# GpSimd takes 384 of 1024 columns of the modulation's sums during the first mixer

## The chip, the core and the metric

The kernel runs on one core of a Trainium2 chip. The metric is the device time of one execution in microseconds, as the median of several runs.

## The reference

The program is a chain of three transformer blocks on a sequence of 256 positions and 1024 channels, all in float32. The first block is conditioned on a vector c by a modulation of six rows:

```
c_act = silu(c)
mod = einsum('bd,de->be', c_act, w_ada) + b_ada          # w_ada: 1024 x 6144
shift_m, scale_m, gate_m, shift_f, scale_f, gate_f = split(mod, 6)
h = rms(x) * (1 + scale_m) + shift_m
proj = h @ w_in                                          # q, k, v, gates of two mixers
fox = forgetting attention, 8 heads of 64;  ret = retention, 4 heads of 128
x = x + gate_m * (concat(fox, ret) @ w_out)
h = rms(x) * (1 + scale_f) + shift_f
x = x + gate_f * (square(relu(h @ w_mlp_in)) @ w_mlp_out)
```

Two further blocks follow (sparse attention with pooling, and gated linear attention), each with its own MLP. The change touches only the product of c_act with w_ada.

## The kernel before

The weights stream from memory in tiles of 128 partitions by 1024 columns (512 KB) through the tensor raw, which has six slots (RAW = 6). The list RAW_SEQ, made by raw_plan, sets the one order in which all tiles pass: ("w", s) is tile s of a weight matrix, ("ada", n) is row block n of w_ada. For a weight tile ScalarE copies raw to whi (hi_to, L581), VectorE writes the rest to wlo (L1107), and TensorE multiplies with both (L1766 to L1768). SyncE (SP) issues the transfers in the order of the list; slot_wait lets tile r go only when raw_done says that tile r - 6 has been used. ScalarE and VectorE work three tiles ahead of TensorE (LEAD = 3).

The modulation is not a TensorE product. For each row block n of w_ada VectorE does one scalar_tensor_tensor (L1130): sums = raw * c_act[block] + sums, where sums is one of six 1024-column pieces of acc. Blocks 0 to 15 (the first two rows of the modulation, in halves, L1117 to L1126) come before the first projections. Blocks 16 to 39 follow one at a time, one behind each weight tile from tile 12 to tile 35; that is the stretch of the first mixer. Blocks 40 to 47 come in the first MLP. When a modulation row's eight blocks are in, mod_bcast on TensorE adds up the partitions (L1854) and ScalarE writes the row back (L609).

Each engine runs its own program in order and waits on semaphores. Between the tiles of w_in the engines do the steps of the mixer, at places fixed by tables (`tiles(T_IN, T_OUT, {...})` on ScalarE and VectorE, `between` on TensorE). On the path of the prediction are: heads_out on ScalarE (L785, the turned and scaled heads; two stand right behind the copy of tile 16), fox_scores on TensorE (L1992, which for the first group waits for four of them), rotate on VectorE (L1390 to L1395) and turn on TensorE (L2110), and quarters of the normalised mixer output (L1757).

GpSimd has little to do. It clears acc, kT and qT, issues a number of transfers (sel, const_c, the gains, decay_c, bands_c, layer norm rows), and computes inverse roots as powers of -1/2 (rsqrt, L467) of up to eight columns, which VectorE asks for (var_ready) and waits for (rstd_ready).

Of the kernel before, what the change touches and what calls it, by code (L numbers as in the profile page):

```python
# [9 lines left out]
ALU = mybir.AluOpType  # L10
AX = mybir.AxisListType.X

P = 128
D = 1024
S = 256
NT = S // P
KC = D // P
# [8 lines left out]
RAW = 6  # L26
# [32 lines left out]

ADA_ORDER = [1, 0, 2, 4, 3, 5]  # L60
ADA_FIRST = 2 * KC


ADA_AFTER = list(range(12, 36))
# [21 lines left out]
ADA_AT = [r for r, (kind, n) in enumerate(RAW_SEQ) if kind == "ada"]  # L86


def raw_full_at(r):

    return 16 * sum(2 if RAW_SEQ[a][0] == "ada" and RAW_SEQ[a][1] < ADA_FIRST else 1 for a in range(r % RAW, r + 1, RAW))


def raw_of(s):
# [4 lines left out]
def units(n):  # L99

    return 4 * (n - 1) - (4 if n > 4 else 0)
# [67 lines left out]
def block_program(nc, dram, out):  # L169
    with ExitStack() as ctx:  # L170
        def sb(name, shape, dt=F32):
            return ctx.enter_context(nc.sbuf_tensor(name, shape, dt))

        def sem(name):
            return ctx.enter_context(nc.semaphore(name))
# [8 lines left out]
        acc = sb("acc", [P, 6 * D])  # L184
# [16 lines left out]
        cvec = sb("cvec", [P, 4, KC])  # L201
# [17 lines left out]
        cred = sb("cred", [P, 4, 16])  # L219
        aT = sc[0:32, 1, 0:S]  # L220
        dec = sb("dec", [P, 4, 4])

        PJ = ctx.enter_context(nc.psum_tensor("PJ", [P, 4, 512], F32))
        AT = ctx.enter_context(nc.psum_tensor("AT", [P, 4, 512], F32))
# [14 lines left out]
        acc_zero, ld_bada, ld_bada2 = sem("acc_zero"), sem("ld_bada"), sem("ld_bada2")  # L239
        xn_done, xt_tr, xt_done, modc_done = sem("xn_done"), sem("xt_tr"), sem("xt_done"), sem("modc_done")  # L240
        h0_hi, h0_32, h0_lo = sem("h0_hi"), sem("h0_32"), sem("h0_lo")
        ada_even = sem("ada_even")
        exp_c = sem("exp_c")
        cast_done = sem("cast_done")
        mod_mm, mod_row = sem("mod_mm"), sem("mod_row")
# [105 lines left out]
        def _(sp):  # L351
            def slot_wait(r):

                if r >= RAW:
                    sp.wait_ge(raw_done, r - RAW + 1)

            def fetch(r, src, view=None):

# [102 lines left out]
        def _(pool):  # L461
            asked = [0]

            def rsqrt(col, n):
                asked[0] += 1
                pool.wait_ge(var_ready, asked[0])
                nc.gpsimd.tensor_tensor(rstd[:, col:col + n], stat[:, col:col + n], nhalf[:, 0:n],  # L467
                                        ALU.pow).then_inc(rstd_ready, 1)
# [25 lines left out]
            bcast(fgain, dram["fox_out_gain"].rearrange("a h d -> (a h d)")).then_inc(ld_mix, 16)  # L494
            bcast(rgain, dram["ret_out_gain"].rearrange("a h d -> (a h d)")).then_inc(ld_mix, 16)
            pool.dma_start(tab[:, 0:1024], dram["decay_c"]).then_inc(ld_mix, 16)
            for t in range(NT):
                rsqrt(S_FO + 8 * t, 8)
            for t in range(NT):
                rsqrt(S_RO + 4 * t, 4)  # L500
            pool.wait_ge(src_ready, units(2))
            pool.dma_start(tab[:, :], dram["bands_c"]).then_inc(ld_tab, 16)

# [576 lines left out]
        def _(dve):  # L1080
# [19 lines left out]
            def raw_to(end):  # L1100

                while nxt[0] < end:
                    r = nxt[0]
                    kind, n = RAW_SEQ[r]
                    if kind == "w":
                        dve.wait_ge(hi_done, n + 1)
                        tt(wlo[:, n % SPL, :], raw_slot(r), whi[:, n % SPL, :].bitcast(F32),  # L1107
                           ALU.subtract).then_inc(raw_done, 1)
                    else:
                        dve.wait_ge(raw_full[r % RAW], raw_full_at(r))  # L1110
                        before, last_ada[0] = last_ada[0], r
                        if n < ADA_FIRST:
                            g, q = divmod(n, 4)
                            even, odd = acc[:, 512 * g:512 * (g + 1)], prT[:, g % 2, :]
                            if q:
                                dve.wait_ge(ada_even, n)
                            stt(even, raw_slot(r)[:, 0:512], cvec[:, 3, 2 * q:2 * q + 1], even, ALU.mult, ALU.add)\  # L1117
                                .then_inc(ada_even, 1)
                            c = cvec[:, 3, 2 * q + 1:2 * q + 2]
                            if q == 0:  # L1120
                                if g >= 2:
                                    dve.wait_ge(mod_mm, g - 1)
                                ts(odd, raw_slot(r)[:, 512:], c, None, ALU.mult).then_inc(raw_done, 1)
                            else:
                                dve.wait_ge(raw_done, before + 1)
                                stt(odd, raw_slot(r)[:, 512:], c, odd, ALU.mult, ALU.add).then_inc(raw_done, 1)  # L1126
                        else:
                            dve.wait_ge(raw_done, before + 1)
                            sums = acc[:, ADA_ORDER[n // KC] * D:(ADA_ORDER[n // KC] + 1) * D]
                            stt(sums, raw_slot(r), cvec[:, 3, n % KC:n % KC + 1], sums, ALU.mult, ALU.add)\  # L1130
                                .then_inc(raw_done, 1)
                    nxt[0] += 1

# [613 lines left out]
        def _(pe):  # L1747
# [101 lines left out]
            def mod_bcast(n, bank0):  # L1849

                pe.wait_ge(raw_done, ADA_AT[KC * n + KC - 1] + 1)
                i = ADA_ORDER[n]
                for j in range(2):
                    ins = mm(AT[:, bank0 + j, :], cst[:, C_TRI + P:C_TRI + 2 * P],  # L1854
                             acc[:, i * D + 512 * j:i * D + 512 * (j + 1)], start=True, stop=True)
                    ins.then_inc(mod_mm, 1)
# [645 lines left out]
```

## Time and profile before

| | |
|---|---|
| median of 3 runs | 1022.15 us |
| the runs | 1015.5, 1022.15, 1022.82 us |
| profiled execution | 1015.01 us, span 1013.2 us |
| TensorE busy | 951.8 us (94%) |
| VectorE busy | 656.6 us (65%) |
| ScalarE busy | 485.2 us (48%) |
| GpSimd busy | 53.9 us (5%) |

The span is what the profiler saw from the first to the last instruction; the execution's own time has 1.8 us around it. Busy shares are means over stages with different limits, so they name no bottleneck by themselves. TensorE's matmuls overlap, and their ends are modelled. "Idle before" is the time an engine stood still ahead of an instruction, with the one that released it.

### The profile page before, as it was taken

The page shows a single profiled execution, that of the slowest core. Times are in us where ns is not written, and L with a number is a line of the kernel's source. Part 1 is how long each engine was busy: PE and PEld are TensorE (multiplying, and loading weights), DVE is VectorE, ACT ScalarE, POOL GpSimd, SP SyncE. Part 2 cuts the span into 40 slices and gives each one's busy share as a digit, 9 for nine tenths or more (in the row PEclk, how much of TensorE's full clock was granted, in tenths as well). Part 3 has the DMA queues.
Part 4 walks back from the last instruction along what each step waited for, and adds up shares of the span by engine and source line. Part 5 has one row for each costly group of instructions (what it writes and reads, how often), then busy time and mean ns, then how long its engine had stood idle before and what let it go on. Part 6 is the DMA issues. An engine that isn't in the chain of part 4 may idle for free.

```text
span 1013.2 us, 14870 instructions
## 1 busy us (share of the span) xinstructions
PE 951.8 (94%) x5572; PEld 816.1 (81%) x5572; DVE 656.6 (65%) x828; ACT 485.2 (48%) x734; POOL 53.9 (5%) x59
## 2 busy tenths in 40 slices
PE   3889979799999999999899999998999989999996
PEld 3767867599999987977689999996776879999995
DVE  5778897886545575666884555558544876554555
ACT  5456646455444444444354544443653735444540
POOL 3030101100000001000020000001000010000000
PEclk9999989999999999999999999999999999999998
DMA  9998776776665576411476556544442447566531
GB/s 285 300 244 287 206 205 231 254 239 220 198 198 185 167 268 153 134 67 59 125 214 230 167 186 201 193 167 147 144 149 100 125 167 249 171 198 206 172 125 42
DMA packets 109991, 186.94 MB, mean 184 GB/s; under 512 B 8696, under 2 KB 67088, under 8 KB 109920
## 3 DMA queue, kind: packets, MB, share of 16 engines
q1 hardware_dynamic: 104800, 177.33, 54.2%
q0 software_dynamic: 2592, 8.53, 3.0%
q8 instruction: 34, 0.56, 0.2%
q10 hardware_dynamic: 2544, 0.35, 0.2%
q14 instruction: 21, 0.17, 0.0%
HBM read 185.13 MB, written 1.05 MB: 184 GB/s over the span
## 4 chain that ended last, share of the span: by engine, by line
PE 78%; DVE 9%; ACT 4%; issue 3%; DMA 2%; POOL 2%; SPq 0%; POOLq 0%; ACTq 0%; DVEq 0%
PE PJ L1766 14%; PE PJ L1767 13%; PE PJ L1768 13%; PE AT L1908 9%; PE AT L1907 9%; PE AT L1906 9%; DVE wlo L1107 2%; POOL rstd L467 2%; PE AT L1992 1%; DMA raw<-in_w_out_dram 1%; PE AT L2035 1%; PE AT L1757 1%; DMA raw<-in_w_in_dram 1%; DVE bn L1192 1%; DVE acc L1130 1%
## 5 line engine op out<-in xcount | busy, mean ns | idle before, releaser
L1107 DVE TENSOR_TENSOR wlo<-raw,whi 128x1024 fp32r<-128x1024 f32 x144 | 172.7, 1220 | 53.4 <-ACT whi L581 52.9
L1906 PE MATMUL AT<-hT_hi,whi 128*128 128x256 f32 x720 | 203.8, 283 | 0.0
L1908 PE MATMUL AT<-hT_hi,wlo 128*128 128x256 f32 x720 | 203.8, 283 | 0.0
L1907 PE MATMUL AT<-hT_lo,whi 128*128 128x256 f32 x720 | 203.7, 283 | 0.0
L1235 DVE TENSOR_TENSOR wlo<-raw,whi 128x1024 fp32r<-128x1024 f32 x144 | 169.8, 1221 | 33.1 <-ACT whi L639 32.6
L1766 PE MATMUL PJ<-whi,uhi 128*128 128x512 f32 x432 | 170.3, 394 | 1.7 <-DVE wlo L1107 0.9
L581 ACT ACTIVATE whi<-raw 128x1024 fp32r<-128x1024 f32 x144 | 146.7, 1054 | 49.4 <-DMA raw<-in_w_in_dram 29.3
L1767 PE MATMUL PJ<-wlo,uhi 128*128 128x512 f32 x432 | 168.7, 390 | 0.0
L1768 PE MATMUL PJ<-whi,ulo 128*128 128x512 f32 x432 | 168.2, 389 | 0.0
L639 ACT ACTIVATE whi<-raw 128x1024 fp32r<-128x1024 f32 x144 | 144.4, 1049 | 48.2 <-PE PJ L1768 44.3
L1766 PE MATMUL PJ<-whi,hT_hi 128*128 128x512 f32 (+1 forms) x320 | 132.3, 413 | 11.4 <-DVE hT_lo L1283 7.3
L1906 PEld LDWEIGHTS AT<-hT_hi,whi 128*128 128x128 f32 x720 | 138.1, 192 | 1.6
L1907 PEld LDWEIGHTS AT<-hT_lo,whi 128*128 128x128 f32 x720 | 138.1, 192 | 1.6
L1908 PEld LDWEIGHTS AT<-hT_hi,wlo 128*128 128x128 f32 x720 | 138.0, 192 | 0.0
L1244 DVE TENSOR_TENSOR pr<-pr 128x512 f32<-128x512 f32 x45 | 31.1, 691 | 161.0 <-ACT pr L649 161.0
L1767 PE MATMUL PJ<-wlo,hT_hi 128*128 128x512 f32 (+1 forms) x320 | 125.2, 391 | 0.0
L1768 PE MATMUL PJ<-whi,hT_lo 128*128 128x512 f32 (+1 forms) x320 | 125.0, 391 | 0.0
L649 ACT ACTIVATE pr<-AT 128x512 f32<-128x512 f32 x45 | 26.8, 597 | 190.0 <-PE AT L1908 190.0
L1766 PEld LDWEIGHTS PJ<-whi,uhi 128*128 128x128 f32 x432 | 81.3, 188 | 20.1 <-issue 2.8
L1768 PEld LDWEIGHTS PJ<-whi,ulo 128*128 128x128 f32 x432 | 81.1, 188 | 17.3
L1767 PEld LDWEIGHTS PJ<-wlo,uhi 128*128 128x128 f32 x432 | 81.3, 188 | 15.2 <-issue 0.2
L1766 PEld LDWEIGHTS PJ<-whi,hT_hi 128*128 128x128 f32 x320 | 61.5, 192 | 30.1 <-DVE hT_lo L1283 8.7
(310 smaller groups left out, 1054.8 us busy)
## 6 DMA issues: line engine op xcount, KB each, us to landing
raw<-in_mlp_w_dram SPq DMA_DIRECT2D x128, 512.0 KB, 4.9
raw<-in_w_in_dram SPq DMA_DIRECT2D x32, 512.0 KB, 6.0
raw<-in_w_ada_dram SPq DMA_DIRECT2D x32, 512.0 KB, 5.0
raw<-in_w_mlp_in_dram SPq DMA_DIRECT2D x32, 512.0 KB, 5.0
raw<-in_w_mlp_out_dram SPq DMA_DIRECT2D x32, 512.0 KB, 5.4
raw<-in_c_w_in_dram SPq DMA_DIRECT2D x24, 512.0 KB, 4.3
raw<-in_w_ada_dram SPq DMA_DIRECT2D x32, 256.0 KB, 6.0
raw<-in_a_w_in_dram SPq DMA_DIRECT2D x12, 512.0 KB, 5.0
```

The lines of the kernel that those rows point to most:

```text
L581: nc.scalar.activation(whi[:, s % SPL, :], raw_slot(r), ACT.Copy).then_inc(hi_done, 1)
L639: nc.scalar.activation(whi[:, s % SPL, :], raw_slot(r), ACT.Copy).then_inc(hi_done, 1)
L649: nc.scalar.activation(pr[:, 0, :], AT[:, j % 2, :], ACT.Relu).then_inc(relu_done, 1)
L1107: tt(wlo[:, n % SPL, :], raw_slot(r), whi[:, n % SPL, :].bitcast(F32), ALU.subtract).then_inc(raw_done, 1)
L1235: tt(wlo[:, s % SPL, :], raw_slot(r), whi[:, s % SPL, :].bitcast(F32), ALU.subtract)\
L1244: tt(pr[:, 1, :], pr[:, 0, :], pr[:, 0, :], ALU.mult).then_inc(usq, 1)
L1766: mm(o, a, hi, start=start, stop=False)
L1767: mm(o, a, lo, start=False, stop=False)
L1768: return mm(o, b, hi, start=False, stop=stop)
L1906: mm(o, whi[:, s % SPL, c], hT_hi[:, k, :], start=first, stop=False, skip_group_check=True)
L1907: mm(o, whi[:, s % SPL, c], hT_lo[:, k, :], start=False, stop=False, skip_group_check=True)
L1908: ins = mm(o, wlo[:, s % SPL, c], hT_hi[:, k, :], start=False, stop=last, skip_group_check=True)
```

## The change

For blocks 16 to 39 VectorE now sums only columns 0 to 639. GpSimd does columns 640 to 1023 with two instructions, since it has no single one for both: share = raw * c_act[block], then sums = sums + share. A new tensor share of 128 x 512 is allocated. A new semaphore ada_pool counts finished shares, ada_prod the products. SP fetches into a slot that held such a block only when both engines are done with it, and TensorE waits for both before it adds up a row. The inverse roots that GpSimd does in this stretch are placed between the shares.

```diff
+ADA_CUT = 640
+ADA_SHARED = range(2 * KC, 5 * KC)
...
+def shared_to(r):
+
+    return sum(1 for n in ADA_SHARED if ADA_AT[n] <= r)
...
                 if r >= RAW:
                     sp.wait_ge(raw_done, r - RAW + 1)
+                    if shared_to(r - RAW) > shared_to(r - RAW - 1):
+                        sp.wait_ge(ada_pool, shared_to(r - RAW))
...
-            for t in range(NT):
-                rsqrt(S_FO + 8 * t, 8)
+            pool.wait_ge(ld_bada2, 16)
+
+            def ada_share(n0, n1):
+
+                for n in range(n0, n1):
+                    r, k = ADA_AT[n], n - ADA_SHARED[0]
+                    pool.wait_ge(raw_full[r % RAW], raw_full_at(r))
+                    if k:
+                        pool.wait_ge(ada_pool, k)
+                    col = ADA_ORDER[n // KC] * D
+                    sums = acc[:, col + ADA_CUT:col + D]
+                    nc.gpsimd.tensor_scalar(share[:, 0:D - ADA_CUT], raw_slot(r)[:, ADA_CUT:],
+                                            cvec[:, 3, n % KC:n % KC + 1], None, ALU.mult).then_inc(ada_prod, 1)
+                    pool.wait_ge(ada_prod, k + 1)
+                    nc.gpsimd.tensor_tensor(sums, sums, share[:, 0:D - ADA_CUT], ALU.add).then_inc(ada_pool, 1)
+
+            ada_share(16, 26)
+            rsqrt(S_FO, 8)
+            ada_share(26, 30)
+            rsqrt(S_FO + 8, 8)
+            ada_share(30, 37)
             for t in range(NT):
                 rsqrt(S_RO + 4 * t, 4)
+            ada_share(37, 40)
...
-                            sums = acc[:, ADA_ORDER[n // KC] * D:(ADA_ORDER[n // KC] + 1) * D]
-                            stt(sums, raw_slot(r), cvec[:, 3, n % KC:n % KC + 1], sums, ALU.mult, ALU.add)\
+                            cut = ADA_CUT if n in ADA_SHARED else D
+                            sums = acc[:, ADA_ORDER[n // KC] * D:ADA_ORDER[n // KC] * D + cut]
+                            stt(sums, raw_slot(r)[:, 0:cut], cvec[:, 3, n % KC:n % KC + 1], sums, ALU.mult, ALU.add)\
...
+                if KC * n in ADA_SHARED:
+                    pe.wait_ge(ada_pool, KC * (n - 1))
```

On GpSimd, from the powers of the q and k heads to the next block's tables, the program before reads as follows (L467 are the powers, L471 broadcasts of a gain row):

```order
L467 TENSOR_TENSOR rstd<-stat,nhalf 128x8 [waits var_ready] x4
L493 DMA cst<-in_const_c_dram 128x512 [waits mod_mm]
L471 DMA acc<-in_fox_out_gain_dram 128x512
L471 DMA tab<-in_ret_out_gain_dram 128x512
L496 DMA tab<-in_decay_c_dram 128x1024
L467 TENSOR_TENSOR rstd<-stat,nhalf 128x8 [waits var_ready] x2
L467 TENSOR_TENSOR rstd<-stat,nhalf 128x4 [waits var_ready] x2
L502 DMA tab<-in_bands_c_dram 128x1536 [waits src_ready]
```

and in the changed program, up to its second share:

```order
L477 TENSOR_TENSOR rstd<-stat,nhalf 128x8 [waits var_ready] x4
L503 DMA cst<-in_const_c_dram 128x512 [waits mod_mm]
L481 DMA acc<-in_fox_out_gain_dram 128x512
L481 DMA tab<-in_ret_out_gain_dram 128x512
L506 DMA tab<-in_decay_c_dram 128x1024
L518 TENSOR_SCALAR share<-raw,cvec 128x384 [waits raw_full5,ld_bada2]
L521 TENSOR_TENSOR acc<-acc,share 128x384 [waits ada_prod]
L518 TENSOR_SCALAR share<-raw,cvec 128x384 [waits ada_pool,raw_full1]
L521 TENSOR_TENSOR acc<-acc,share 128x384 [waits ada_prod]
```

The first share stands behind the four powers and the four transfers; ten shares then run ahead of the next power.

On SP, the transfers from the tile of sum 16 on in the changed program (L371 is the fetch, L361 before; before, all of these wait for raw_done alone):

```order
L371 DMA raw<-in_w_ada_dram 128x1024 [waits raw_done]
L371 DMA raw<-in_w_in_dram 128x2x512 [waits raw_done]
L371 DMA raw<-in_w_ada_dram 128x1024 [waits ada_pool,raw_done]
L371 DMA raw<-in_w_in_dram 128x2x512 [waits raw_done]
L371 DMA raw<-in_w_ada_dram 128x1024 [waits ada_pool,raw_done]
L371 DMA raw<-in_w_in_dram 128x2x512 [waits raw_done]
```

From the tile of sum 19 on, each w_ada tile waits for GpSimd too, and the weight tile behind it stands in the same queue.

## Rows read from the trace of the kernel before

**Rows 1.** The page, part 1: busy us, share of span, instructions

```profile
PE 951.8 (94%) x5572; PEld 816.1 (81%) x5572; DVE 656.6 (65%) x828; ACT 485.2 (48%) x734; POOL 53.9 (5%) x59
```

**Rows 2.** Table of stretches: length, then each engine's busy us, clock, DMA share

```profile
95.00:115.00 20.00, 20.00 (x119) 17.59 (x118) 13.54 (x16) 13.38 (x36) 0.00 (x0) 1.00 0.90 232
115.00:143.00 28.00, 22.76 (x111) 17.82 (x110) 26.85 (x41) 17.50 (x25) 4.64 (x2) 0.95 0.65 199
...
205.00:400.00 195.00, 193.87 (x1211) 174.79 (x1209) 120.89 (x122) 90.57 (x111) 4.12 (x3) 1.00 0.63 203
```

**Rows 3.** Tile raw, 60 to 205 us: duration ns min/median/max, first and last start

```profile
L1130 DVE SCALAR_TENSOR_TENSOR acc<-raw,cvec,acc x24: 1273/1276/1285, 69.2 to 177.6; 128x1024 f32<-128x1024 f32 x24
...
DMA to landing us min/median/max: 3.2/5.4/10.2
```

**Rows 4.** Tile acc, 0 to 420 us, the same columns

```profile
L1117 DVE SCALAR_TENSOR_TENSOR acc<-raw,cvec,acc x16: 733/742/750, 9.1 to 53.6; 128x512 f32<-128x512 f32 x16
```

**Rows 5.** GpSimd's instructions in time: start us, us, engine, line, operation

```profile
0.78 1.80 POOL L474 MEMSET acc<- 128x2048 f32 x1
7.38 0.55 POOL L467 TENSOR_TENSOR rstd<-stat,nhalf 128x1 f32<-128x1 f32 x1 [4.80 <-DVE stat L1161]
...
8.84 3.51 POOL L477 MEMSET acc<- 128x4096 f32 x1
...
77.45 0.54 POOL L496 DMA_DIRECT2D tab<-in_decay_c_dram  x1
115.45 2.63 POOL L467 TENSOR_TENSOR rstd<-stat,nhalf 128x8 f32<-128x8 f32 x1 [37.45 <-DVE stat L1161]
...
193.42 1.48 POOL L467 TENSOR_TENSOR rstd<-stat,nhalf 128x1 f32<-128x1 f32 x1 [16.14 <-DVE stat L1161]
```

**Rows 6.** VectorE's instructions in time

```profile
116.47 1.23 DVE L1107 TENSOR_TENSOR wlo<-raw,whi 128x1024 fp32r<-128x1024 f32 x1
117.62 0.68 DVE L1390 TENSOR_TENSOR sc<-PJ,cst 128x512 f32<-128x512 f32 x1
...
171.50 0.69 DVE L1226 SCALAR_TENSOR_TENSOR proj<-PJ,proj 128x512 f32<-128x512 f32 x1 [0.51 <-ACT proj L624]
...
193.25 1.22 DVE L1107 TENSOR_TENSOR wlo<-raw,whi 128x1024 fp32r<-128x1024 f32 x1
```

**Rows 7.** SP's issues in time

```profile
70.56 0.34 SPq L361 DMA_DIRECT2D raw<-in_w_ada_dram  x1
71.69 0.37 SPq L361 DMA_DIRECT2D raw<-in_w_in_dram  x1
```

**Rows 8.** ScalarE's instructions in time

```profile
80.53 1.06 ACT L581 ACTIVATE whi<-raw 128x1024 fp32r<-128x1024 f32 x1
81.61 1.26 ACT L785 ACTIVATE kT<-AT,qkgain 64x512 f32<-64x512 f32 x2
```

**Rows 9.** TensorE's instructions in time

```profile
84.20 1.05 PE L1992 MATMUL AT<-kT,qT 104*128 104x128 f32 x8
...
94.55 0.63 PE L2004 MATMUL AT<-cst,pr 128*128 128x128 f32 x4 [0.95 <-ACT kT L785]
...
140.70 1.08 PE L2110 MATMUL AT<-cst,proj 128*128 128x128 f32 x4 [4.03 <-DVEq L1396]
```

**Rows 10.** Table of stretches, two microseconds behind that idle time

```profile
142.00:144.00 2.00, 1.06 (x5) 1.10 (x6) 1.74 (x3) 0.42 (x1) 0.00 (x0) 0.50 0.03 8
```

**Rows 11.** The chain that ended last, 55 to 210 us: start us, us, what

```profile
176.56 8.72 DMA raw<-in_w_out_dram
```

**Rows 12.** Groups of VectorE's instructions, 115 to 143 us: busy us, mean ns, idle before

```profile
L1130 DVE SCALAR_TENSOR_TENSOR acc<-raw,cvec,acc 128x1024 f32<-128x1024 f32 x6 | 7.7, 1281 | 0.5 <-DVE proj L1395 0.5
L1107 DVE TENSOR_TENSOR wlo<-raw,whi 128x1024 fp32r<-128x1024 f32 x5 | 6.1, 1219 | 0.0
L1395 DVE TENSOR_TENSOR proj<-sc 128x512 f32<-128x512 f32 x4 | 2.8, 693 | 0.1
...
L1371 DVE TENSOR_TENSOR proj<-proj,acc 128x512 f32<-128x512 f32 x2 | 1.4, 692 | 0.1
```

More of the change, by code:

```diff
@@ L221, in block_program @@
         dec = sb("dec", [P, 4, 4])
+        share = sb("share", [P, 512])
         PJ = ctx.enter_context(nc.psum_tensor("PJ", [P, 4, 512], F32))
@@ L241, in block_program @@
         h0_hi, h0_32, h0_lo = sem("h0_hi"), sem("h0_32"), sem("h0_lo")
-        ada_even = sem("ada_even")
+        ada_even, ada_prod, ada_pool = sem("ada_even"), sem("ada_prod"), sem("ada_pool")
         exp_c = sem("exp_c")
```

## The prediction, made before the changed kernel ran

> **What bounds the kernel now.** The stage table of the page comes first: over the whole span VectorE is busy 65%, so its work as such buys nothing [rows 1]. The table of stretches says where it does: from 205 us on TensorE is busy 193.87 of 195.00 us, and from 95 to 115 us all of the time; only from 115 to 143 us does it stand at 22.76 of 28.00 while VectorE is at 26.85 [rows 2]. That is the first mixer. What is gained or lost there is passed on whole, because nothing behind 205 us has room to take it up or to give it back.
>
> Who waits there? TensorE has its one long idle time before 140.70 us, 4.03 us, and what ends it is VectorE (the rotated queries of retention) [rows 9]. The view of instructions in time shows VectorE working without a gap up to that point. So the modulation's sums (L1130) that it does on the way count in full in this stretch, and nearly nowhere else.
>
> **The change, part by part.**
>
> *VectorE's shorter instruction.* All 24 sums that start between 69.2 and 177.6 us shrink from 1024 to 640 columns. One takes 1276 ns at 1024 columns [rows 3], the 512-column form 742 ns [rows 4]. The slope is 534 / 512 = 1.04 ns a column, so 384 columns are 0.40 us; for 24 that is 9.6 us, the most that the change could ever bring, 0.9% of the span. Between 95 and 115 us TensorE hides it: cover, no gain. In 115 to 143 us six sums start, the last at the very end, and five lie ahead of the step TensorE waits for [rows 12]: **-2.0 us**. In the tail, the chain passes through the transfer of a w_out tile, which is issued at 176.56 us, when a sum frees its slot, and lands 8.72 us later [rows 11]: one sum, -0.4 us.
>
> *GpSimd's two instructions, 24 times.* The trace shows no large GpSimd arithmetic. Its nearest rows are the two memsets: 1.80 us for 2048 columns, 3.51 for 4096, or 0.835 ns a column written [rows 5]. 384 columns are 0.32 us for the product (one input). The sum has two inputs; if it reads them one after the other, 0.64 us (below: 0.32, if both come at once; above: twice that, 1.28). What stands around it: a power of one column takes 0.55 us with VectorE quiet [rows 5], of which I take 0.43 as fixed, since with VectorE in the way it ends 0.43 after the obstacle (next part). A share is thus 0.75 + 1.07 = 1.8 us, at a supply of one tile per 4 to 5 us. GpSimd keeps up, once it has started. The Trainium skill (GPSIMD Engine Reference, Performance versus the Vector engine) gives 4497 ns for an add of 2048 columns; scaled to 384 an estimate from it is 0.84 us, in place of my 0.64 and 0.43. No row here shows such an add.
>
> *The port.* The power of one column at 193.42 us took 1.48 us, not 0.55. VectorE ran a 1.22 us subtraction with both inputs in SBUF from 193.25 to 194.47; GpSimd ended 0.43 later [rows 5, 6]. So GpSimd does wait for such an instruction to end. The other direction is not so clear. At 115.45 an 8-column power waited in the same way and ran on to 118.08, while VectorE's next subtraction ran from 116.47 in its usual time (1.23 us) and its successor began 1.15 later, as always [rows 5, 6]. VectorE was not held while GpSimd computed; it can have been held for 8 reads at most, too little to see. With 384 columns the reads last as long as the instruction streams. I take it that GpSimd, once waiting, gets in between two VectorE instructions (as at 116.5) and holds the next two-input one while it reads: 0.32 + 0.64 = 0.96 us a share. How much of VectorE's time is exposed: L1130 5 x 1.28, L1107 6.1, L1395 2.8, and three groups of 1.4 us like L1371 have both inputs in SBUF [rows 12], together 19.5 of 28 us, 0.70. The eight shares 26 to 33 fall here: 8 x 0.70 x 0.96 = **+5.4 us** (bounds: 0, if both engines read side by side; 8 x 0.70 x 1.82 = +10.2, if the whole instruction holds the port).
> By the Trainium skill (SBUF — State Buffer, Who interferes with whom) whichever instruction starts first has the pair for the whole instruction. The row of GpSimd waiting agrees; the 8-column row, where VectorE ran beside it, does not. By that rule the term would be the +10.2 of the bound.
>
> *The late start.* This is the wait that the change adds on the queue of transfers. A slot is refilled only when GpSimd is through with it too. When VectorE has done sum 16, SP issues the tile of sum 19 into its slot, at 70.56 us, and tile 16 of w_in next, at 71.69 [rows 7]. But GpSimd's program reaches its first share only after two powers and four DMA issues, at 77.45 + 0.54 = 78.0 us [rows 5], some 0.4 earlier with the shorter sum ahead of the powers. With 1.8 us for the share and about 0.5 us before each of its halves for a VectorE instruction to end, SP gets on at 80.4, and tile 16, queued behind, is issued at 80.8: 9.1 us late. Landing takes 5.4 us in the median, 3.2 at least [rows 3]: 86.2. ScalarE's copy of that tile stands at 80.53 us [rows 8], and behind it on ScalarE stand the turned heads (81.61), without which TensorE's first attention scores at 84.20 can't start [rows 9]. From copy to heads done it is 2.34 us: scores at 88.5, 4.3 late. Of it the 0.95 us that TensorE later waits anyway (94.55) is taken back [rows 9]: **+3.4 us**. Below: with no port waits and a 3.2 us landing +0.3. The slack behind it does not swallow the rest, since 95 to 115 us is TensorE at its limit and VectorE's gapless stretch begins from what TensorE and ScalarE hand it. Above: after the idle 4.03 us the granted clock is 0.50 from 142 to 144 us, the 1.2 GHz level [rows 10]; a new idle time of that length could be followed by the same, and at half speed for 4 to 5 us cost some 2 us more.
>
> *The other moved steps.* The four inverse roots stand between shares now. The first is asked at 115.45 us [rows 5], and VectorE uses its result four tiles later in its program: hidden. Share 26 stands behind it and ends about 3 us after VectorE's own part, but the tile fetched into its slot is used six places later in the sequence: hidden too, by that lead; without it this would be paid like the late start. Shares 37 to 39 run just ahead of the end of the mixer: 3 x 0.70 x 0.96 = +2.0, less two sums' 0.8 and the 0.51 us that VectorE waits for ScalarE there [rows 6], +0.7. With the -0.4 of the tail: **+0.3 us**. TensorE's wait on the new counter is met before VectorE's own.
>
> Sum: -2.0 + 5.4 + 3.4 + 0.3 = **+7.1 us**. Against the profiled execution's 1015.01 us: 1022.1. The other runs took 1015.5, 1022.15 and 1022.82, so the same kernel moves by 7 us from one execution to the next. The median, 1022.15, is of the upper pair; three new runs may have theirs in either. I set the sum against the mean of the four, 1018.9: **1026 us**.
>
> **The rivals.**
> - *The reads pass side by side.* VectorE is never held. What speaks for it is the subtraction at 116.47, unhurt. Left are the late start without port waits (share done at 79.4, tile 16 issued at 79.8, +2.4), -2.0 and -0.4: 0.0, so 1019. Chance 0.25.
> - *Whole-instruction hold.* Port term +10.2, the tail +1.5 in place of +0.3, late start +5.4 with the slow clock: 10.2 + 1.5 + 5.4 - 2.0 = +15, so 1034. Against it is the 8-column row, which however was computing, not reading. The skill's rule quoted above is this case. Chance 0.15.
> - *The late start costs nothing and the sums pay* (the other side). With the four GpSimd DMAs through by 80 us, the transfers then issued have the queues to themselves and land in 3.2 us; the ScalarE step slips under TensorE's tile work, and the VectorE savings ahead of 115 us count too. With about ten sums of the chain in the mixer at 0.40 us: -4, so 1015. It decides if tile 16 lands before about 82 us, for which GpSimd would have to be at its first share by 76 us; the DMA issues stand against that. Chance 0.10.
>
> The forecast as summed has the remaining 0.50.
>
> **How the numbers follow.** The forecast's terms alone span +3 to +12. With the base between 1015.3 and 1022.5 the side-by-side case reaches down to 1014 or so, and the forecast's upper end and half of the whole hold up to 1035. The range is 1014 to 1035; out of it are most of the faster case on the lower base and the whole hold on the upper. One per cent of the median, about what a measurement of this kernel can tell from no change, is 10 us, which is more than the change can bring if every sum lay on the path: faster 0.04, only by the spread of runs; slower, above 1032.4, is the whole hold and the top of the forecast: 0.17; within 0.79.
>
> **What the new profile would show.** VectorE's sums near 880 ns, if not held; means above that, or subtractions (L1107's) above 1.22 us beside GpSimd's reads, show the port. GpSimd's first product near 77.6 us, and an idle time of TensorE of 3 to 5 us ahead of the first scores near 84 us, show the late start; the transfer of w_in's tile 16 should be issued near 80 us. TensorE's wait before the rotated queries longer than 4.03 us means that the port cost more than the sums gave. The prediction is wrong if VectorE's instructions keep their times and TensorE does not stop near 84 us, or if GpSimd's add takes several microseconds, when slots come free late all through the mixer.

## The result

The changed kernel takes 1024.51 us (median of 11 runs, 1021.32 to 1027.23), the kernel before 1016.69 us in 11 runs taken with them (1014.24 to 1022.82). The ratio is 1.0058 [1.0038, 1.0077], or +5.9 us [3.9, 7.8] by the ratio; the two medians alone lie 7.8 us apart. So it is slightly slower and stays within the 1% that the prediction called no change. 1026 us was predicted. Of the three runs shown ahead of the prediction, two lie at the upper end of the kernel's spread. Eleven runs have their median at 1016.69, 5.5 us below the 1022.15 of those three.

The profiled execution took 1024.3 us, +9.3 on the profiled one of before, where the sum of terms said +7.1. Every measured difference below is a ratio less one, multiplied with the median of before. The two medians by themselves can lie up to 1.5 us off it: the kernel with the gain alone is 2.7 us faster by the ratio and 1.2 by the medians.

### The profile after

The page's first part, to be read against [rows 1]:

```profile
PE 955.8 (93%) x5572; PEld 820.2 (80%) x5572; DVE 657.6 (64%) x828; ACT 485.4 (47%) x734; POOL 124.7 (12%) x107
```

GpSimd has 48 instructions more and is busy 71 us longer. VectorE is given 9.6 us of work less and is still busy 1.0 us longer. The table of stretches, with the columns of [rows 2] (length, busy us of TensorE, its weight loads, VectorE, ScalarE and GpSimd, clock, DMA share, GB/s):

```profile
115.00:143.00 28.00, 26.42 (x133) 21.22 (x131) 24.92 (x33) 19.69 (x31) 19.00 (x12) 1.00 0.63 194
...
84.00:88.00 4.00, 0.00 (x0) 0.00 (x0) 1.73 (x2) 1.91 (x3) 3.66 (x4) 1.00 1.04 376
88.00:92.00 4.00, 3.54 (x18) 3.28 (x19) 3.64 (x4) 1.80 (x3) 3.75 (x3) 0.57 0.97 348
```

TensorE does nothing at all from 84 to 88 us, where it had begun the attention scores before, and the four microseconds behind that run at a granted clock of 0.57, mostly at the 1.2 GHz level. That is the late start. (The stretch from 115 to 143 us looks better for TensorE only because its wait has moved out of it.) The chain of waits from 76 to 92 us shows how the idle time comes about (start us, us, what):

```profile
76.98 1.85 POOL share L518
...
78.91 1.94 POOL acc L521
...
80.92 0.34 SPq L371
...
81.30 4.74 DMA raw<-in_w_in_dram
...
87.14 1.26 ACT kT L815 x2
...
88.45 0.61 PE AT L2018
```

Read it downwards: GpSimd's first share, product and sum, ends at 80.85 us (78.91 + 1.94). SP then issues the w_ada tile at 80.92 and tile 16 of w_in at 81.30, against 70.56 and 71.69 before [rows 7]. Tile 16 lands at 86.04; ScalarE copies it and makes the heads; TensorE starts. ScalarE's row of the copy names the transfer as what it waited for, and the scores' own row (L2025 below) may be laid beside the 84.20 of [rows 9], so they start 4.66 us late:

```profile
86.06 1.06 ACT L611 ACTIVATE whi<-raw 128x1024 fp32r<-128x1024 f32 x1 [6.61 <-DMA raw<-in_w_in_dram]
```

```profile
88.45 0.61 PE L2018 MATMUL AT<-negb,identb 128*128 128x512 bf16 x1 [5.38 <-ACT kT L815]
88.86 1.91 PE L2025 MATMUL AT<-kT,qT 104*128 104x128 f32 x8
...
99.37 0.60 PE L2037 MATMUL AT<-cst,pr 128*128 128x128 f32 x4
...
147.51 1.09 PE L2143 MATMUL AT<-cst,proj 128*128 128x128 f32 x4 [6.03 <-DVEq L1427]
```

The row at 99.37 is the step that stood at 94.55 before [rows 9]: 4.8 us late. The last row is the wait for the rotated queries, 6.03 us where it was 4.03, now ending at 147.51 in place of 140.70, so 6.8 us late. What VectorE lost on the way shows in the two engines' instructions in time, from 125 to 132 us. GpSimd:

```profile
125.92 1.02 POOL L521 TENSOR_TENSOR acc<-acc,share 128x384 f32<-128x384 f32 x1
127.11 2.67 POOL L518 TENSOR_SCALAR share<-raw,cvec 128x384 f32<-128x384 f32 x1 [0.17 <-POOL acc L521]
129.87 1.02 POOL L521 TENSOR_TENSOR acc<-acc,share 128x384 f32<-128x384 f32 x1
```

VectorE, beside it:

```profile
126.02 1.60 DVE L1161 SCALAR_TENSOR_TENSOR acc<-raw,cvec,acc 128x640 f32<-128x640 f32 x1 [0.23 <-DVE proj L1426]
127.55 1.21 DVE L1137 TENSOR_TENSOR wlo<-raw,whi 128x1024 fp32r<-128x1024 f32 x1
128.68 1.12 DVE L1161 SCALAR_TENSOR_TENSOR acc<-raw,cvec,acc 128x640 f32<-128x640 f32 x1
130.31 1.66 DVE L1137 TENSOR_TENSOR wlo<-raw,whi 128x1024 fp32r<-128x1024 f32 x1 [0.51 <-ACT whi L611]
```

A free sum of 640 columns takes 0.88 us, a free subtraction 1.22. The sum at 126.02 starts when GpSimd's add has 0.92 us to go, and is 0.72 late. The subtraction at 130.31 starts when an add has 0.58 to go, and is 0.44 late. The product at 127.11 is another matter. It waits until VectorE's subtraction ends at 128.76 (2.67 us in place of a free 1.24) and gets in before the next sum. It then runs on until 129.78, 1.1 us of it beside that sum, and costs the sum only 0.24. Over tile raw from 60 to 210 us (duration ns, min, median, max):

```profile
L1161 DVE SCALAR_TENSOR_TENSOR acc<-raw,cvec,acc x24: 868/892/1645, 68.6 to 184.6; 128x640 f32<-128x640 f32 x24
L518 POOL TENSOR_SCALAR share<-raw,cvec x24: 1242/1554/2894, 77.0 to 180.2; 128x384 f32<-128x384 f32 x24
```

The median sum is 892 ns against 1276 [rows 3], so most are not held, and the maximum says what a held one costs. To have one number for each kernel, called the held time below, I took each VectorE instruction from 60 to 215 us, subtracted the duration of its form when GpSimd stands still, and added up what is over 0.1 us. Before: none. After: 9.96 us in 18 instructions, 0.87 at most; 4.45 us of it from 112 to 152 us.

**Where the +9.3 of the profiled pair lies.** One set of TensorE matmuls in the first MLP starts at 211.17 before and at 217.71 after, +6.5:

```profile
211.17 0.60 PE L1885 MATMUL AT<-cst,pr 128*128 128x128 f32 x4
```

```profile
217.71 0.60 PE L1918 MATMUL AT<-cst,pr 128*128 128x128 f32 x4
```

A step in the second block is at 489.52 and 498.79: +9.3, and there it stays to the end. The 2.7 us in between come where neither kernel has any of the changed work. The granted clock from 400 to 450 us differs:

```profile
400.00:450.00 50.00, 49.09 (x329) 40.88 (x328) 29.95 (x57) 22.53 (x54) 0.00 (x0) 0.97 0.41 130
```

in the kernel before, and after:

```profile
400.00:450.00 50.00, 49.76 (x306) 42.01 (x304) 29.93 (x53) 23.19 (x53) 1.13 (x2) 0.90 0.49 132
```

The first experiment below has 0.90 there as well (in 50 us that are shifted by 3 us against these), although it is ahead until then, and loses 2.8 us between the same two steps. The kernel with the first share moved, which carries all the work of the change, has 0.97 there and loses nothing. Nor is this the only such stretch: four of the profiled executions below (the port alone, no shares for the first three blocks, two adds, the cut at 832) lose another 3.1 to 3.3 us between 700 and 900 us, at 0.98 in place of 1.00. So one profiled pair tells +6.5 for the mixer, near the +5.9 of the runs, and 2.7 for a clock that differs far behind the change. With one trace of each kernel it isn't shown whether the change has a part in that clock. The start of that step near 211 us is a second measure for every kernel below; I give it as "step at 211", from one execution each, without an interval.

### The profile page after: what moved, and what is told of

It reads as the page before. It is cut to its first block, busy times and chain, and to the rows that moved or that the text cites. A ratio compares the mean times of both kernels' runs of the same rounds, so it can differ in the third digit from the quotient of the medians.

```text
span 1022.5 us, 14966 instructions
## 1 busy us (share of the span) xinstructions
PE 955.8 (93%) x5572; PEld 820.2 (80%) x5572; DVE 657.6 (64%) x828; ACT 485.4 (47%) x734; POOL 124.7 (12%) x107
## 3 DMA queue, kind: packets, MB, share of 16 engines
HBM read 185.13 MB, written 1.05 MB: 182 GB/s over the span
## 4 chain that ended last, share of the span: by engine, by line
PE 80%; DVE 8%; ACT 4%; issue 3%; DMA 2%; POOL 2%; ACTq 0%; POOLq 0%; SPq 0%; DVEq 0%
PE PJ L1797 14%; PE PJ L1798 14%; PE PJ L1799 14%; PE AT L1941 8%; PE AT L1940 8%; PE AT L1939 8%; PE AT L2025 2%; POOL rstd L477 1%; DVE wlo L1137 1%; DMA raw<-in_w_in_dram 1%; PE AT L2037 1%; PE AT L1788 1%; DVE bn L1223 1%; DVE x L1221 1%; DMA raw<-in_w_out_dram 1%
## 5 line engine op out<-in xcount | busy, mean ns | idle before, releaser
L477 POOL TENSOR_TENSOR rstd<-stat,nhalf 128x1 f32<-128x1 f32 (+2 forms) x22 | 25.9, 1183 | 643.5 <-DVE stat L1229 511.8
```

## The experiments

All were timed in five rounds against the kernel before; the intervals are about 2 us either way. "The port" is short for whatever GpSimd and VectorE share when both work in SBUF. My theory was that of the prediction: a small gain, a larger loss by the port, and a late start. Rivals: that reads pass side by side, or that GpSimd's whole instruction holds VectorE.

### The gain alone

```diff
-                            sums = acc[:, ADA_ORDER[n // KC] * D:(ADA_ORDER[n // KC] + 1) * D]
-                            stt(sums, raw_slot(r), cvec[:, 3, n % KC:n % KC + 1], sums, ALU.mult, ALU.add)\
+                            cut = 640 if 2 * KC <= n < 5 * KC else D
+                            sums = acc[:, ADA_ORDER[n // KC] * D:ADA_ORDER[n // KC] * D + cut]
+                            stt(sums, raw_slot(r)[:, 0:cut], cvec[:, 3, n % KC:n % KC + 1], sums, ALU.mult, ALU.add)\
```

> The kernel before, with VectorE's sums 16 to 39 cut to 640 columns and nobody doing the other 384 (their part of the modulation is left out). It is the gain alone. Theory (gain -2.4, port +5.7, late start +3.4 to +5): 2 to 3 us faster than before, the rotated queries at 138 to 139 us instead of 140.70, TensorE's wait there 2 us shorter than 4.03. Rival (the sums are hidden everywhere, so the change could only cost): no change. Rival (about ten sums of the chain count): 4 us faster.

Columns 640 to 1023 of these sums are left out, so this kernel is for timing alone. 0.9973 [0.9955, 0.9991], or -2.7 us; step at 211 -3.1. The wait for the rotated queries is 3.06 us in place of 4.03 and ends at 139.02, 1.7 us sooner; the other 1.4 us come between there and the step at 211. This is what the spared columns bring if they cost nothing elsewhere: 2.7 of the 9.6 us that VectorE is spared.

### The port alone

```diff
-                    if shared_to(r - RAW) > shared_to(r - RAW - 1):
-                        sp.wait_ge(ada_pool, shared_to(r - RAW))
...
-                    nc.gpsimd.tensor_scalar(share[:, 0:D - ADA_CUT], raw_slot(r)[:, ADA_CUT:],
+                    nc.gpsimd.tensor_scalar(share[:, 0:D - ADA_CUT], cst[:, 0:D - ADA_CUT],
...
-                    nc.gpsimd.tensor_tensor(sums, sums, share[:, 0:D - ADA_CUT], ALU.add).then_inc(ada_pool, 1)
+                    nc.gpsimd.tensor_tensor(share[:, 0:D - ADA_CUT], cst[:, 0:D - ADA_CUT], share[:, 0:D - ADA_CUT],
+                                            ALU.add).then_inc(ada_pool, 1)
...
-                            cut = ADA_CUT if n in ADA_SHARED else D
+                            cut = D
```

> GpSimd does its 48 instructions of 384 columns at the same places, but reads a constant tile and writes a scratch tile; VectorE does all 1024 columns; SP and TensorE do not wait for GpSimd. Only the port is left of the change. Theory (GpSimd's reads hold VectorE's next instruction with two inputs in SBUF): 5 to 8 us slower than before, first scores still near 84 us, rotated queries near 146, subtractions beside GpSimd up to 0.9 us longer. Rival (reads side by side, the loss is all from the queue): within 1 us of before, all VectorE durations as before.

1.0071 [1.0047, 1.0095], or +7.2 us; step at 211 +7.4. The scores start at 84.95, so at most 0.8 us of this is a late start. By the rotated queries (145.59) the kernel is 4.9 us late; 2.5 us more are lost in the tail, between there and the step at 211. GpSimd, then VectorE, in time:

```profile
126.98 1.18 POOL L519 TENSOR_TENSOR share<-cst,share 128x384 f32<-128x384 f32 x1
```

```profile
127.23 2.01 DVE L1136 TENSOR_TENSOR wlo<-raw,whi 128x1024 fp32r<-128x1024 f32 x1
```

The subtraction starts 0.93 us before the add ends and takes 0.79 more than its 1.22. GpSimd works on other tensors than VectorE here, so it is the port and no wait. The held time is 12.25 us in 24 instructions, 5.6 of it from 112 to 152 us. The wait for the rotated queries doubles to 8.07 us. The rival of reads that pass side by side is refuted.

### Writes alone

As the last, but GpSimd clears 896 columns of share (0.84 to 0.87 us each in the trace) in place of each of its two instructions.

> As the run on the port alone, but each of the 48 instructions is a memset of 896 columns, 0.85 us by the slope of the memsets: GpSimd is as long at work and writes more, but reads nothing. Theory (it is the reads): within 1 us of before. Rival (a busy GpSimd is enough, as its powers come later, or its writes hold VectorE): as slow as the run on the port alone.

1.0006 [0.999, 1.0022]: +0.6 us; step at 211 +0.7. No VectorE instruction from 60 to 215 us is held; the sums and subtractions of tile raw, 60 to 210 us:

```profile
L1134 DVE TENSOR_TENSOR wlo<-raw,whi x32: 1215/1219/1228, 61.1 to 207.3; 128x1024 fp32r<-128x1024 f32 x32
L1158 DVE SCALAR_TENSOR_TENSOR acc<-raw,cvec,acc x25: 1273/1279/1286, 69.8 to 208.4; 128x1024 f32<-128x1024 f32 x25
```

So what costs is not that GpSimd writes. It is busy 1.7 us a share here and 2.2 with product and add; the two kernels differ in that and in the reads, and the kernels with two products and two adds below tell the two apart.

### The waits alone

The changed kernel, with GpSimd's two instructions cut to 8 columns each and every semaphore in place (the other 376 columns are left out):

```diff
-                    nc.gpsimd.tensor_scalar(share[:, 0:D - ADA_CUT], raw_slot(r)[:, ADA_CUT:],
+                    nc.gpsimd.tensor_scalar(share[:, 0:8], raw_slot(r)[:, ADA_CUT:ADA_CUT + 8],
...
-                    nc.gpsimd.tensor_tensor(sums, sums, share[:, 0:D - ADA_CUT], ALU.add).then_inc(ada_pool, 1)
+                    nc.gpsimd.tensor_tensor(sums[:, 0:8], sums[:, 0:8], share[:, 0:8], ALU.add).then_inc(ada_pool, 1)
```

> The changed kernel with all its waits, VectorE at 640 columns, but GpSimd's two instructions do 8 columns each (the other 376 are left out). Theory: the port costs next to nothing, the late start stays, only shorter: first share done near 78 us instead of 80.8, tile 16 of w_in issued near 78.5, first scores near 86 us; with the gain of 2.4 within 1.5 us of before. Rival (the port makes nothing, the queue everything): most of the 6.5 us by which the first MLP starts late stays.

1.0016 [0.9998, 1.0034], or +1.6 us; step at 211 +3.1. With the gain of 2.7 (by the step 3.1) in it, the late start is worth about 4.3 by the runs and 6.1 by the step. But the place of the scores was missed: they start at 89.19, as late as in the changed kernel, though each share has next to no work. GpSimd in time:

```profile
76.72 1.61 POOL L518 TENSOR_SCALAR share<-raw,cvec 128x8 f32<-128x8 f32 x1
78.42 1.02 POOL L521 TENSOR_TENSOR acc<-acc,share 128x8 f32<-128x8 f32 x1
79.61 0.31 POOL L518 TENSOR_SCALAR share<-raw,cvec 128x8 f32<-128x8 f32 x1 [0.17 <-POOL acc L521]
80.00 0.20 POOL L521 TENSOR_TENSOR acc<-acc,share 128x8 f32<-128x8 f32 x1
```

Free, the two take 0.31 and 0.20 us; the first pair stood behind two-input instructions of VectorE and took 1.61 and 1.02. So the first share takes 2.7 us here, 2.2 of it waiting; in the changed kernel it takes 3.9. To leave out nearly all of the columns saves only 1.2 us. Tile 16 is issued at 79.91, 1.4 us sooner than in the changed kernel, yet ScalarE gets it at 86.40, 0.3 us later: six tiles are issued between 79.52 and 82.64, where the changed kernel issues two by then, and tile 16 takes 6.5 us to land in place of 4.74. So the size of the first share changes the scores' start little here; the next experiment moves its place.

### The first share earlier

GpSimd's program is put in another order: the first share behind two of the four powers, three more behind the others, and the four transfers last.

```diff
-            for c in (S_FQ, S_FK):
-                rsqrt(c, 8)
-                rsqrt(c + 8, 8)
-            pool.wait_ge(mod_mm, 4)
...
-            ada_share(16, 26)
+            rsqrt(S_FQ, 8)
+            rsqrt(S_FQ + 8, 8)
+            ada_share(16, 17)
+            rsqrt(S_FK, 8)
+            rsqrt(S_FK + 8, 8)
+            ada_share(17, 20)
+            pool.wait_ge(mod_mm, 4)
+            pool.dma_start(cst[:, C_MIX:], dram["const_c"][:, C_MIX:C_SBUF]).then_inc(ld_mix, 16)
...
+            ada_share(20, 26)
```

> The changed kernel with GpSimd's first shares moved ahead: share 16 behind the two powers of the q heads, shares 17 to 19 behind those of the k heads and ahead of its four transfers. All work and all waits are kept; only the late start goes. Theory: tile 16 of w_in issued near 71 us instead of 81.3, first scores near 84 instead of 88.5, 4 to 5 us faster than the changed kernel, and still 3 to 5 us slower than before, by the port (+7.2) less the sums (-2.7). Rival (the late start is swallowed by TensorE's later idle time): as slow as the changed kernel, +0.6%.

1.0023 [1.0003, 1.0043], or +2.3 us; step at 211 +2.8. SP's row of tile 16 and TensorE's of the scores are back where they were before (71.69 and 84.20):

```profile
71.64 0.37 SPq L371 DMA_DIRECT2D raw<-in_w_in_dram  x1
```

```profile
84.48 1.05 PE L2028 MATMUL AT<-kT,qT 104*128 104x128 f32 x8
```

By this kernel the late start is worth 5.9 - 2.3 = 3.6 us (by the step at 211, 3.7); the two intervals leave it between 1 and 6. It isn't the late start alone that the edit moves. The four transfers now go out from 85.16 us on, 9.4 us later than in the kernel before, and a w_in tile issued at 87.07, just behind them, takes 11.02 us to land (6.2 before). ScalarE and then TensorE wait for it:

```profile
98.11 1.06 ACT L614 ACTIVATE whi<-raw 128x1024 fp32r<-128x1024 f32 x1 [2.21 <-DMA raw<-in_w_in_dram]
```

```profile
99.80 1.08 PE L2132 MATMUL AT<-proj,prT 128*128 128x64 f32 x8 [1.66 <-ACT prT L807]
```

The kernel before has no such wait, so the late start may be worth more than 3.6. The +2.3 that stay are less than the 4.5 that the port's 7.2 and the gain's 2.7 make, but the difference is within the intervals. The trace has less held time too: 10.2 us in 20 instructions against 12.25 in 24 of the port-only kernel, and from 112 to 152 us 4.3 against 5.6. Why fewer are held isn't shown.

### No shares for the first three blocks

Shares from block 19 on alone (21 of 24), so that the first falls behind VectorE's sum 18.

> The changed kernel with sums 16 to 18 left to VectorE whole; GpSimd takes part from sum 19 on, and waits once for VectorE's sum 18. Theory: as the run with the early share: the slots that gate tile 16 and 17 of w_in no longer wait for GpSimd; 3 to 5 us slower than before, first scores near 84 us. Rival: the late start only moves to the next tiles, +0.5% and more.

1.0 [0.9979, 1.0021]: 0.0 us; step at 211 +2.2, scores at 84.23. It removes the late start by another way and leaves the four transfers where they were; three shares less are done. Against the changed kernel it is 5.9 us faster by the runs and 4.3 by the step. The two measures differ by 2 us, so whether this one is a little better than the last stays open. It is no gain over the kernel before.

### Which of the two instructions costs

The port-only kernel with two products, and with two adds, in place of one of each (both read constants and write share).

> As the run on the port alone, but both GpSimd instructions of each share are products (one input, 1.24 us when nothing is in the way). Theory (VectorE is held while GpSimd reads: about 0.3 us by a product, 0.8 by an add, as the stretched VectorE instructions of the port run show): 0.6 in place of 1.1 us a share, so about 4 us slower than before against 7.2. Rival (the whole instruction holds the port, 1.24 and 0.99 us): more than the 7.2 of the run with one of each.

> As the run on the port alone, but both GpSimd instructions of each share are adds of two SBUF inputs (0.99 us when nothing is in the way). Theory (held while GpSimd reads): 1.6 us a share, about 10 us slower than before. Rival (the whole instruction): 1.98 in place of 2.23 us a share, so less than 7.2.

Two products: 1.0004 [0.9985, 1.0023], +0.4 us; step at 211 +2.3. I expected about 4. The held time is 4.68 us in 18 instructions, never more than 0.32 us, beside GpSimd products that last 1.24 us free. One of them, GpSimd and then VectorE (1.28 us free):

```profile
125.29 1.35 POOL L516 TENSOR_SCALAR share<-cst,cvec 128x384 f32<-128x384 f32 x1 [0.17 <-POOL share L519]
```

```profile
125.45 1.60 DVE L1160 SCALAR_TENSOR_TENSOR acc<-raw,cvec,acc 128x1024 f32<-128x1024 f32 x1
```

Two adds: 1.014 [1.0109, 1.017], +14.3 us, step at 211 +14.0, more than the 10 I expected: a held time of 18.45 us in 31 instructions, 0.85 at most, and a wait for the rotated queries of 9.75 us, ending at 152.29. VectorE from 143 to 150 us, where GpSimd does five such adds one behind the other; four instructions of 0.69 or 1.22 us free:

```profile
143.39 2.01 DVE L1138 TENSOR_TENSOR wlo<-raw,whi 128x1024 fp32r<-128x1024 f32 x1
145.33 1.48 DVE L1401 TENSOR_TENSOR proj<-proj,rstd 128x512 f32<-128x512 f32 x1
146.84 1.36 DVE L1403 TENSOR_TENSOR proj<-proj,acc 128x512 f32<-128x512 f32 x1
148.24 1.36 DVE L1405 TENSOR_TENSOR proj<-proj 128x512 f32<-128x512 f32 x1
```

Two products are busy for longer than product and add (2.5 us a share against 2.2) and cost less, two adds for less time (2.0) and cost more. So it is not the time at work that counts. One input holds VectorE for a quarter of the product's time, two inputs nearly until the add ends. The rival of the whole instruction is refuted for the product (1.24 us, 0.32 held) and nearly right for the add (1.00 us, up to 0.87 held).

### A smaller share

```diff
-ADA_CUT = 640
+ADA_CUT = 832
```

> The changed kernel with the cut at column 832: GpSimd takes 192 columns in place of 384. Theory: the gain halves (-1.4), the add's hold halves to about 0.4 us and with it the port's cost (about 3.6), and the late start stays nearly whole (3 to 4 us, since what makes it is the place of the first share, not its length): 5 to 6 us slower than before. Rival (the cost goes with the columns alone): half of the changed kernel's 5.9, so 3 us.

1.0059 [1.0042, 1.0077], or +6.0 us, as much as with twice the columns; step at 211 +6.1. The held time falls with the columns, to 3.4 us in 12 instructions and 0.42 at most, and the gain falls too: VectorE's sum takes 1.07 us. The late start stays whole (tile 16 issued at 82.21, scores at 90.01). GpSimd's free durations here, 0.77 us for the product and 0.59 for the add of 192 columns, lie on the lines through 0.31 and 0.20 (8 columns) and 1.24 and 1.00 (384): 2.5 and 2.1 ns a column.

### The other way round: GpSimd's clears off VectorE

The trace of before holds one case in which GpSimd already costs VectorE time. These two kernels went after it; they carry none of the change.

```diff
+            nc.gpsimd.memset(acc[:, 2 * D:], 0.0).then_inc(acc_zero, 1)
             rsqrt(S_N1, 1)
             rsqrt(S_N1 + 1, 1)
-            nc.gpsimd.memset(acc[:, 2 * D:], 0.0).then_inc(acc_zero, 1)
```

> The kernel before, with GpSimd clearing the last 4096 columns of acc ahead of the first two powers (while it waits) in place of behind them; nothing else. In the trace of before VectorE's first product (L1123, one SBUF input) takes 2.87 us while that memset runs, against 0.48 us for its three like later on. Theory (a write of GpSimd holds that form of VectorE instruction too): the first product takes 0.48 us, the first sums reach TensorE 2.4 us sooner, and the kernel is up to 2.4 us faster. Rival (transfers pace the first 60 us, so the time is taken back): L1123 short, the time the same within 0.5 us.

The second has this too, and lets the clear of kT wait until VectorE has begun on h:

```diff
             pool.wait_ge(rstd_ready, 2)
+            pool.wait_ge(h0_lo, 1)
             nc.gpsimd.memset(kT[64:P, :], 0.0).then_inc(acc_zero, 1)
```

> As the run that clears acc first, and the memset of kT (64 partitions by 2048, 1.80 us, which had come to lie on VectorE's first product there: 1.93 us in place of 0.48) waits until VectorE has written the first low half of h, near 20 us. Theory (a GpSimd write holds VectorE's one-input product to the end of the memset): L1123 at 0.48 us all four times, the first sums reach TensorE near 13.6 us in place of 15.99, up to 2.4 us faster than before, and faster than the run with acc cleared first (-1.9). Rival: the time is the transfers' and nothing more is gained than by that run.

0.9981 [0.996, 1.0001] and 0.9979 [0.9958, 1.0]: -1.9 and -2.1 us, each with an interval that touches no change. The traces are plainer than the times. VectorE's first product of the modulation (raw times c_act, one input, 512 columns), before:

```profile
9.76 2.87 DVE L1123 TENSOR_SCALAR prT<-raw,cvec 128x512 f32<-128x512 f32 x1
...
25.86 0.48 DVE L1123 TENSOR_SCALAR prT<-raw,cvec 128x512 f32<-128x512 f32 x1
```

with the large clear out of the way:

```profile
9.68 1.93 DVE L1123 TENSOR_SCALAR prT<-raw,cvec 128x512 f32<-128x512 f32 x1
```

and with the second one, of kT, away as well:

```profile
9.86 0.48 DVE L1124 TENSOR_SCALAR prT<-raw,cvec 128x512 f32<-128x512 f32 x1
```

The 2.87 us end 0.28 us behind the clear of 4096 columns, which runs from 8.84 to 12.35 [rows 5]; the 1.93 end 0.28 us behind the clear of kT, which here runs from 9.53 to 11.33. By the Trainium skill (SBUF — State Buffer, Who interferes with whom) this form can enter a mode that takes the pair shared with GpSimd, and the later of two then blocks fully; the rows agree. TensorE's step at 211 comes 1.0 and 3.7 us sooner. By that step the last is the fastest kernel of this study, but between it and the kernel before, the runs cannot quite decide.

## Why the prediction was right

**What bounds the kernel.** Borne out. In the kernel with the gain alone TensorE is 0.7 us ahead from its first scores to 136 us and 1.7 at the rotated queries. So the spared columns count in VectorE's stretch and not from 95 to 115 us; from the step at 211 to 400 us its lead doesn't change. Of the 9.6 us spared, 2.7 came through (predicted 2.4), but not where it was forecast: by the steps 1.7 up to the rotated queries, 1.0 of it in the stretch (predicted 2.0), and 1.4 in the tail (predicted 0.4).

**The late start.** Borne out nearly to the number: first share at 76.98 (predicted 77.6), done at 80.85 (80.4), tile 16 issued at 81.30 (80.8), landed at 86.04 (86.2), scores at 88.86 (88.5). Its price is where it is less sure. 3.4 us was predicted; taking it away brings 3.6 us in one kernel and 5.9 in the other (by the step 3.7 and 4.3), and left alone in the kernel it is worth about 4.3 (6.1). So 3.4 is at the low end. The slow clock named as the upper bound did come: 0.57 from 88 to 92 us. The forecast had left it out of the sum, and had taken 0.95 us off for an idle time that TensorE has later anyway. That idle time is gone, but the slow clock costs as much: the scores' eight matmuls take 1.91 us in place of 1.05, the scores are 4.7 us late and the step at 99.37 still 4.8, where 3.4 was expected.

**The port.** The mechanism holds: GpSimd waits for VectorE's two-input instruction to end, gets in ahead of the next and holds it. That it does so just as long as it reads is a reading of the two lengths, not shown by itself. By the trace 4.45 us are held from 112 to 152 us (5.4 predicted), the adds carrying most. How the 0.96 us a share was made up is only half right. The 0.32 for the product is what the product-only kernel shows as its most. The 0.64 for the add was too little at its worst, with up to 0.87 measured. And the product itself lasts 1.24 us, not 0.75; the price of a memset's column was the wrong row for it. It did little harm to the sum: two products a share, 2.5 us of GpSimd's time, cost +0.4 us (step at 211 +2.3). The add was predicted at 1.07 and takes 1.00. The estimate from the Trainium skill (GPSIMD Engine Reference, Performance versus the Vector engine), 0.84, is further off than that 1.07, which had the fixed time of a power added.

By the Trainium skill (SBUF — State Buffer, Who interferes with whom) a VectorE instruction with two inputs in SBUF contends with a GpSimd instruction that reads SBUF and not with one that only writes it. The clears that hold nothing (+0.6 us) agree. It calls the pair an exclusive lock, and says of VectorE's two-port modes that whoever issues first has it for the whole instruction; the prediction carried that over to instructions with two inputs. The add nearly does so (0.87 of 1.00 us), the product does not (0.32 of 1.24).

**The tail and the other moved steps.** The changed kernel is 6.8 us late at the rotated queries and 6.5 at the step at 211, so the tail gives back 0.3 us where +0.3 was predicted. Its parts are larger than forecast and nearly cancel: the shorter sums alone gain 1.4 us there, the port alone costs 2.5.

**The sum.** +7.1 was predicted; the runs say +5.9 [3.9, 7.8] and the step at 211 +6.5. The parts measured alone, -2.7, +7.2 and +3.6, make 8.1, which is not clear of 5.9 given intervals of some 2 us on each.

Step by step the sum is right in part by luck. At the rotated queries it had -2.0 + 5.4 + 3.4 = +6.8, and 6.8 was measured. But 4.8 of that stood already at 99.37, where 3.4 was forecast, and VectorE's stretch then added 2.0, where -2.0 + 5.4 = 3.4 was. The late start was put 1.4 us too low, for the most part by the slow clock that the sum left out, and what the shares cost in the stretch as much too high, and the two errors cancel.

**What was off** is the base. The prediction set the sum on 1018.9, the mean of four executions, and 11 runs have it at 1016.69. By the base it was 2.2 us too high, and the medians of 11 runs lie 7.8 apart where it had 7.1; so 1026 came 1.5 us above 1024.51. The statement that nothing behind 205 us takes up or gives back time is right from the step at 211 to 400 us, where every kernel keeps its distance to 0.1 us. Behind that the granted clock differs between profiled executions, worth up to 2.8 us from 400 to 450 us and up to 3.3 from 700 to 900. Why it does stays open.

**The rivals.** Side by side: refuted (port alone +7.2). The whole instruction: refuted for the product and in size, since it asked for +15. The late start costing nothing: refuted, as TensorE idles from 84 to 88 us and taking the late start away brings 3.6 us or more back.

## What to carry to other kernels

Before work moves to an idle engine, price it by what that engine's reads hold on the busy one: here each add of 384 columns on GpSimd held VectorE for up to 0.87 us to save it 0.40, and in all 24 shares 9.96 us were held for 9.6 spared. None of the shared versions tried here paid, and the best only drew level. Then look at where the first new instruction stands in its engine's queue and whose buffers it sits on. A slot is free when its slowest reader is through, and the transfer behind it in the queue, which had nothing to do with the change, was 9.6 us late. And judge an effect of half a per cent by a step soon behind the change as well as by the end, since a later stage may run at another clock; where the two differ by 2 us, as they do for two kernels here, claim no more than both bear out.

## What the runs showed of the hardware

- GpSimd, float32, 128 partitions, free of VectorE: a product with one input and a scalar per partition takes 0.31, 0.77 and 1.24 us for 8, 192 and 384 columns; an add with two inputs 0.20, 0.59 and 1.00. The product is the slower of the two, though it reads half as much.
- The product of 384 columns holds VectorE's two-input instructions by at most 0.36 us (port alone, at 179.32; 0.32 with two products a share) and the add by at most 0.87. A memset of 896 columns (0.84 us) holds them not at all.
- A memset does hold VectorE's one-input product (tensor_scalar from SBUF to SBUF), to 0.28 us past its end: 2.87 and 1.93 us in place of 0.48. That is the opposite of the last point.
- A product of 8 columns on GpSimd took 1.61 us in place of 0.31 with VectorE's two-input work ahead of it. Where others wait for GpSimd, leaving out columns doesn't take that part of its price away.
